# Routing chunks 0 to 5 at the chunk loop's ninth step, with a first tile of expert 0 computed while chunks 6 and 7 are routed

## The reference, cut to what is computed

```python
def moe(x, router_w, router_b, w_gate, w_up, w_down):
    xt = x.reshape(B_ * S_, D_)
    s = jax.nn.sigmoid(xt.astype(jnp.float32) @ router_w.astype(jnp.float32))
    sel = s + router_b.astype(jnp.float32)
    gscore = lax.top_k(sel.reshape(-1, N_GROUPS, EXPERTS_PER_GROUP), 2)[0].sum(-1)
    gidx = jnp.argmax(gscore, axis=-1)
    in_group = (jnp.arange(N_EXPERTS) // EXPERTS_PER_GROUP)[None, :] == gidx[:, None]
    _, eidx = lax.top_k(jnp.where(in_group, sel, -jnp.inf), TOP_K)
    gate = jnp.take_along_axis(s, eidx, axis=1)
    gate = gate / gate.sum(-1, keepdims=True)
    ...
    for e in range(N_EXPERTS):
        hid = jax.nn.silu(xt @ w_gate[e]) * (xt @ w_up[e])
        out = out + combine[:, e:e + 1] * (hid @ w_down[e])
...
x = layer_norm(DEEPNORM_ALPHA * x + y, ln1_w[l], ln1_b[l])   # y: the mixer's output
y = moe(x, router_w, router_b, w_gate[l], w_up[l], w_down[l])
x = layer_norm(DEEPNORM_ALPHA * x + y, ln2_w[l], ln2_b[l])
```

## Time and profile before

| what | value |
| --- | --- |
| median of 3 runs | 950.18 us (949.54 to 957.41) |
| span of the profiled execution | 950.0 us |
| TensorE busy | 925.5 us, 97% of the span |
| VectorE busy | 633.3 us, 67% |
| ScalarE busy | 459.2 us, 48% |
| GpSimd busy | 208.8 us, 22% |
| instructions | 15583 |

### The profile page before, as it was taken

How to read it: one execution, slowest core, us unless ns; L and a number is a source line. 1 busy time by engine, 2 the same in 40 slices (tenths; PEclk the granted TensorE clock), 3 DMA queues, 4 the chain that set the end, 5 groups by cost and what they waited for, 6 DMA issues and landing times.

```text
span 950.0 us, 15583 instructions
## 1 busy us (share of the span) xinstructions
PE 925.5 (97%) x5174; PEld 799.9 (84%) x5174; DVE 633.3 (67%) x965; ACT 459.2 (48%) x631; POOL 208.8 (22%) x229
## 2 busy tenths in 40 slices
PE   8999999999999999999889999999999999999997
PEld 8998887888777788888678898898898898898884
DVE  3433599896328877677874389486689983517487
ACT  4532101010348634532515479476788974536653
POOL 3100000010121000000021543524353642324230
PEclk9999999999999999999999999999999999999997
DMA  8620304111563544445386889879699998838264
GB/s 286 205 96 29 100 33 144 45 45 56 197 216 111 203 157 176 163 156 199 137 308 178 267 285 372 309 252 389 183 372 390 390 390 247 290 67 302 75 223 177
DMA packets 72965, 195.20 MB, mean 205 GB/s; under 512 B 9582, under 2 KB 23488, under 8 KB 72928
## 3 DMA queue, kind: packets, MB, share of 16 engines
q1 hardware_dynamic: 60976, 156.43, 45.0%
q0 software_dynamic: 11808, 38.15, 14.5%
q10 hardware_dynamic: 144, 0.14, 0.1%
HBM read 159.47 MB, written 35.22 MB: 205 GB/s over the span
## 4 chain that ended last, share of the span: by engine, by line
PE 90%; DVE 4%; issue 2%; ACT 2%; DMA 1%; POOL 1%; SPq 0%; POOLq 0%; DVEq 0%; ACTq 0%
PE banks L1294 14%; PE banks L684 14%; PE banks L673 13%; PE banks L699 13%; PE banks L1291 9%; PE banks L1434 9%; PE banks L1358 4%; PE banks L657 2%; PE banks L1466 1%; PE banks L664 1%; PE banks L732 1%; DVE split_weights L1885 1%; PE banks L1412 1%; PE banks L1409 1%; DMA arena<-sum_scratch 1%
## 5 line engine op out<-in xcount | busy, mean ns | idle before, releaser
L766 DVE TENSOR_TENSOR split_weights<-arena,split_weights 128x1024 fp32r<-128x1024 f32 x192 | 223.2, 1219 | 0.0
L762 ACT ACTIVATE split_weights<-arena 128x1024 fp32r<-128x1024 f32 x192 | 190.9, 1056 | 3.8 <-DMA arena<-in_w_down 2.0
L684 PE MATMUL banks<-split_weights,split_rows 128*128 128x256 f32 x1152 | 147.5, 284 | 0.0
L684 PEld LDWEIGHTS banks<-split_weights,split_rows 128*128 128x128 f32 x1152 | 142.7, 191 | 1.9
L1294 PE MATMUL banks<-split_weights 128*128 128x512 f32 (+2 forms) x768 | 136.3, 338 | 1.7 <-DVE split_weights L1742 1.6
L699 PE MATMUL banks<-split_weights,split_hidden 128*128 128x512 f32 x576 | 137.5, 394 | 0.0
L673 PE MATMUL banks<-split_weights,split_rows 128*128 128x512 f32 x576 | 136.2, 393 | 0.7 <-DVE split_rows L949 0.7
L1294 PEld LDWEIGHTS banks<-split_weights 128*128 128x128 f32 x768 | 118.7, 189 | 17.6 <-DVE split_weights L1736 2.1
L673 PEld LDWEIGHTS banks<-split_weights,split_rows 128*128 128x128 f32 x576 | 109.2, 190 | 23.6 <-issue 0.8
L699 PEld LDWEIGHTS banks<-split_weights,split_hidden 128*128 128x128 f32 x576 | 106.5, 188 | 21.6
L587 POOL DMA_INDIRECT sum_scratch<-work,tile_sums x23 | 85.0, 3694 | 110.7 <-ACT work L816 101.8
(11 more groups left out here) (349 smaller groups left out, 1117.0 us busy)
## 6 DMA issues: line engine op xcount, KB each, us to landing
arena<-in_w_gate SPq DMA_DIRECT2D x64, 512.0 KB, 7.2
arena<-in_w_up SPq DMA_DIRECT2D x64, 512.0 KB, 7.1
arena<-in_w_down SPq DMA_DIRECT2D x64, 512.0 KB, 10.0
arena<-in_w_in SPq DMA_DIRECT2D x20, 512.0 KB, 5.3
arena<-in_x SPq DMA_DIRECT2D x16, 512.0 KB, 6.8
arena<-in_w_out SPq DMA_DIRECT2D x8, 512.0 KB, 5.0
x_scratch<-arena SPq DMA_DIRECT2D x8, 512.0 KB, 3.5
sum_scratch<-arena SPq DMA_DIRECT2D x8, 512.0 KB, 4.5
```

The lines of the kernel that those rows point to most:

```text
L684: last = pe.matmul(bank(up_bank[a])[:, 0:DH2], XR[:, hx, k, :], wu[:, hw, k, a * DH2:(a + 1) * DH2], start=(k == 0 and i == 0), stop=(k == ...
L762: act.activation(unit_split(u, 0), unit_slot(u), AF.Copy).then_inc(xw_hi, 1)
L766: dve.tensor_tensor(unit_split(u, 1), unit_slot(u), unit_split(u, 0).bitcast(F32), ALU.subtract).then_inc(xw_lo, 1)
```

## The change

**Ninth step.** ScalarE takes the exponential of the logits of chunks 0 to 5 (AHEAD = T - 2 = 6), and VectorE chooses for these chunks (`choose`, a new function: it finds the two best of four by comparing all pairs, in 25 instructions). TensorE sums the ranks of experts 0 and 1 over these chunks (`first_ranks`) ahead of the router product of chunk 6. VectorE no longer casts `ones`, makes `stri` and subtracts units 2 and 3 in this step: GpSimd does these (its subtraction of units 2 and 3 signals `xw_lo`).

**Tenth step.** VectorE makes the one-hot rows of expert 0's first 128 tokens (`first_one_hots`) ahead of the last residual, and their list `tok1` (`first_indices`) behind it, with TensorE's sum between (`first_tokens`). GpSimd gathers these rows, and subtracts units 4 to 7. ScalarE rounds units 4 and 5 here.

**Behind the loop.** TensorE transposes the gathered rows and multiplies the first tile, outside of the loop over tiles (`first_gate`, `first_up`, `first_hidden`, `first_down`). VectorE splits the rows, then chooses for chunks 6 and 7, and then runs what it ran before behind the choice, with the steps of the first tile set in between (`hidden`, `first_hidden_lo`). TensorE's ranks of all chunks stand between two blocks of the gate product; the sum for expert 0's second tile (`second_tokens`, `tok2`) stands in the up product. GpSimd gathers the second tile when `tok2` is there, and then subtracts units 8 to 11; after these it raises `xw_lo` by 8, gathers the first tile's gates and loads the rows ln2_w and ln2_b. A number `room` is added to the ranks of chunks 6 and 7 where expert 0's first tile isn't full. The one-hot sum stands behind the first tile's down product, and TensorE reads `ntiles` behind it. The loop over tiles begins with tile 1.

The core of the diff (the new functions of TensorE's first tile repeat the products of `body` for tile 0):

```diff
@@ pool_experts
-            pool.wait_ge(x1_out, PRIMED + 32 * T)
+            def first_expert_lo(*units):
+                for u in units:
+                    pool.wait_ge(xw_hi, u + 1)
+                    pool.tensor_tensor(unit_split(u, 1), unit_slot(u), unit_split(u, 0).bitcast(F32), ALU.subtract).then_inc(w_lo, 1)
+            pool.wait_ge(xr_lo, T)
+            pool.tensor_copy(ones_bf, ones[:, :])
+            pool.tensor_tensor(stri, tri[:, :], ident[:, :], ALU.subtract).then_inc(made, 1)
...
+            for i, u in enumerate((2, 3)):
+                pool.wait_ge(xw_hi, i + 1)
+                pool.tensor_tensor(unit_split(u, 1), unit_slot(u), unit_split(u, 0).bitcast(F32), ALU.subtract).then_inc(xw_lo, 1)
+            pool.wait_ge(x1_out, PRIMED + 32 * AHEAD)
             pool.wait_ge(rows_filled, 48)
             pool.wait_ge(first_tok_ready, 1)
+            pool.indirect_dma_start(out=xe, out_offset=None, in_=x1_dram[0:P + AHEAD * P, :],
+                                    in_offset=bass.IndirectOffsetOnAxis(ap=tok1, axis=0)).then_inc(xe_in, 16)
+            pool.tensor_copy(tok_gate, tok1).then_inc(gate_idx_ready, 1)
+            first_expert_lo(4, 5, 6, 7)
+            pool.wait_ge(x1_out, PRIMED + 32 * T)
+            pool.wait_ge(first_tok_ready, 2)
+            pool.wait_ge(xeT_ps, 1)
             pool.indirect_dma_start(out=xe, out_offset=None, in_=x1_dram,
-                                    in_offset=bass.IndirectOffsetOnAxis(ap=tok1, axis=0)).then_inc(xe_in, 16)
-            pool.wait_ge(tok_ready, 1)
-            gather(1)
+                                    in_offset=bass.IndirectOffsetOnAxis(ap=tok2, axis=0)).then_inc(xe_in, 16)
+            pool.sem_inc(idx_ready, 1)
+            first_expert_lo(8, 9, 10, 11)
+            pool.wait_ge(w_lo, PROJECTED + 8)
+            pool.wait_ge(xw_lo, 4)
+            pool.sem_inc(xw_lo, 8)
             pool.wait_ge(gates_out, 16)
...
@@ pe_experts
+            stay_busy(8)
             pe.wait_ge(xe_in, 16)
...
+            stay_busy(10)
+            pe.wait_ge(xw_lo, 4)
+            pe.wait_ge(first_lo, 1)
+            first_gate(range(KC // 2))
+            pe.wait_ge(xe_lo, 1)
+            first_gate(range(KC // 2, KC - 1))
+            ranks()
+            first_gate(range(KC - 1, KC)).then_inc(gate_ps, 1)
+            first_up(0, range(KC // 2))
+            second_tokens()
+            first_up(0, range(KC // 2, KC)).then_inc(up_ps, 1)
+            first_up(1, range(KC // 2))
+            first_hidden(0)
+            first_up(1, range(KC // 2, KC)).then_inc(up_ps, 1)
+            transpose_rows(1)
+            first_hidden(1)
+            first_down(range(FC)).then_inc(y_ps, 1)
             pe.wait_ge(hot_ready, 1)
...
-            pe.wait_ge(xw_lo, 4)
+            pe.wait_ge(ntiles_ready, 1)
+            counts = tile_counts(pe, "pe")
             each_tile(pe, counts, body)
@@ act_experts
+            act.wait_ge(y_ps, 1)
+            act.wait_ge(y_out, ADDED)
+            act.wait_ge(gate_in, 16)
+            act.activation(ys, psum[:, 2:4, :].rearrange("p a n -> p (a n)"), AF.Copy, scale=gate_rows[:, 0:1]).then_inc(y_sb, 1)
@@ VectorE, step of the chunk loop
+                if n == T + 1:
+                    first_one_hots(dve, own)
                 if norms:
                     residual1(ch.plus(-2), 1)
+                    if n == T + 1:
+                        first_indices(dve, own)
...
+                if n == T:
+                    dve.wait_ge(rt_exp, 1)
+                    dve.wait_ge(small_in, 16 * SMALL_LOADS)
+                    choose(dve, own, 0, AHEAD)
                 if projects:
...
-                if n == T:
-                    dve.tensor_copy(ones_bf, ones[:, :])
-                    dve.tensor_tensor(stri, tri[:, :], ident[:, :], ALU.subtract)
-                    for i, u in enumerate((2, 3)):
-                        expert_lo(dve, 0, u, i + 1)
```

289 lines of the change are left out of this document (199 added, 90 removed).

## The result

The changed kernel takes 969.53 us (median of 4 runs, 967.17 to 971.6), the kernel before 953.23 beside it; the ratio is 1.0163 with a 95% interval of 1.0135 to 1.0191. The forecast was 952.0 with a range up to 957. The profiled execution of the changed kernel has a span of 965.8 us, 15.8 more than the 950.0 of before.

A forecast was written before the change was run, and what follows sets the result against it. TensorE, busy 97%, was taken as the bound, so the start S of tile 1's gate product decides: 950.0 + 504.5 - 502.53 = 952.0 us, VectorE and GpSimd taking turns; range 939.5 to 957.

The forecast's parts named there:

- S: Instant at which tile 1's gate product can begin: 502.53 us before, forecast 504.5; the same 23 tiles follow.
- Steps 1 and 2: Choice for six chunks ready at 453.9 us, slowed by GpSimd's units 2 and 3; first tokens tok1 ready at 457.5.
- Step 3: First gather at 459.5 us; unit 4's subtraction delays chunk 7's scaling, which ends at 463.8; unit 5 ends at 465.5.
- Step 4: Chunk 7's transposes and router product take 2.7 us as before, ending at 466.5; first tile's rows split by 470.4.
- Step 5: Choice for two chunks, 3.5 us alone, begins at 470.4 and, slowed by GpSimd's subtractions, is ready at 478.3.
- Step 6: From the second choice to the second tokens 3.5 us: tok2 at 481.9, counts and a tile product done by 484.4.
- Step 7: Second gather 482.8 to 483.9 us, units 8 to 11 until 494.0; VectorE's four small instructions pass one at a time.
- Steps 8 and 9: VectorE's remaining work to the last one-hot at 502.7 us; one-hot sum and counters, 1.74 plus 0.1, give S 504.5.
- The down product: First tile's down product, 5.5 us, waits for the last hidden product until 495.8 and ends at 501.3, just ahead.
- Side by side: Rival, chance 0.25: VectorE and GpSimd don't block each other; S 489.9 or 491.7, 2.6 lost to ln2 load, 940.0 us.
- TensorE stays at 1.2 GHz: Rival, chance 0.12: half clock from waits for ranks and hidden rows until tile 1's first product; 962 us.
- Only one-input instructions are blocked: Rival, chance 0.13: GpSimd's subtractions hold up only VectorE's one-input instructions; S = 494.5, 942 us.

The follow-up runs named there:

- fill: The changed kernel with 12 more TensorE filler products where it waited between 452 and 465 us; ratio to the kernel before 1.0104.
- early: The changed kernel with VectorE's choice for chunks 6 and 7 made ahead of splitting the first tile's rows; ratio to the kernel before 1.0106.
- turns: The changed kernel with GpSimd's units 9 to 11 each waiting until the previous is stored, and unit 6 until 7 is rounded; ratio to before 1.0156.
- fence: The changed kernel with GpSimd copying one column behind the second gather and waiting until it is stored, before unit 8; not timed, profiled span 959.8 us.
- short_all: The changed kernel with each of GpSimd's ten subtractions cut from 1024 to 32 columns; ratio to the kernel before 0.9926.
- gather_last: The changed kernel with GpSimd's second gather moved behind its subtractions of units 8 to 11; not timed, profiled span 974.0 us.
- best3: The changed kernel with units 8 to 11 on VectorE, earlier second choice, 12 fillers, GpSimd's units 2 to 7 later, counters read earlier; ratio to before 0.9976.
- alldve2: The changed kernel with all ten subtractions on VectorE behind what TensorE waits for, earlier second choice, ranks and counters; ratio to the kernel before 0.9940.

## Why the prediction was wrong

**What bounds the kernel: right.** S decided, and the same 23 tiles follow it; the span follows S but for the end and tile 1's clock.

**Steps 1 and 2 (choice, first tokens): right.** Shifted by 0.48 to the clock of the kernel after, the choice was due at 453.4 and came at 453.13, tok1 was due at 457.0 and came at 456.85.

**Step 3 (units 4 and 5, x1): a term too small.** The x1 scaling is two instructions, L2221 x2, and each waited for a subtraction: it ended at 464.88, not 463.3. I had let only the first wait. 1.6 us.

**Step 4 (router, first rows): the largest mistake.** The rows were split at 475.94, due 469.9: 6.0 late. 1.6 are step 3's. Nearly all the rest is TensorE's half clock, which held from 454 to 475: router, fillers and transposes, one behind the other, cost nearly twice what they cost at 2.4 GHz (3.23 against fill's 1.75, 3.60 against 1.96), where the forecast took the price of before, 1.97 for the router. The clock was among the rivals, but only from the ranks on; TensorE's waits begin earlier, at 452. Fill, whose rows were split 4.1 earlier, shows that the clock alone was worth about 4 us.

**Step 5 (second choice): right.** 7.75 us from 475.86 to 483.61, 7.9 forecast, only late by step 4. That it could stand ahead of the rows I did not see; early shows 3.3 to 5.4 us in it.

**Step 6: late by a further us.** tok2 came at 488.17, due 481.4; 0.9 beyond step 5 is the half clock in the up products just ahead.

**Step 7 (turns at units 8 to 11): wrong in kind.** That "each GpSimd subtraction lets one VectorE instruction of that kind through" held for units 2 to 7 and not behind the gather. The end of the last subtraction was due at 493.5 and came at 499.23, 5.7 late: they began at 489.99 instead of 483.4, and took 9.24 together instead of 10.1. What failed is what VectorE had done by then: nothing, so that its last one-hot ended at 512.06, 12.8 us behind the subtractions' end where 8.6 were forecast. One instruction of 9.45 us where four turns had been counted: 4 us, a part of which (in turns and fence all but about 1 us) returns as other waits.

**Steps 8 and 9 (counters, S): too small by 1.7.** The one-hot sum is 0.64 and the stretch of the counters behind it 2.79; I had 1.8 for both.

**The down product** was no bound: it ended at 511.1, ahead of the one-hots. **Tile 1's gate product** was taken at full clock and ran at 1.2 GHz for a part: 1.9.

Together: 5.7 for the end of the subtractions, 4.2 for what was left to do then, 1.7 for the counters, 11.6 in all. S was due at 504.0 on this clock and came 11.5 later.

**The rivals.** *Side by side* had 940.0; short_all, which comes near it, has a span of 942.5 and S at 493.65, with the second gather, 5.18 us, on its chain. The sum without the ports was off by 2.5 us only, but in part by luck: counted from the choice, S came 4.1 us later than its 489.9 (2.4 later than its 491.7), and tile 1's gate product took 8.23 us instead of 5.44; against that, the 2.6 for the ln2 load were not lost, though ScalarE did wait 7.60 us for that load, and the end behind the tiles was 1.3 shorter. The larger part of the mistake lies in the price of the ports and of the clock. *TensorE stays at 1.2 GHz* (962) had the right cause in the wrong place, and I gave it 0.12. *Only one-input instructions are blocked* is refuted, by TENSOR_TENSOR rows of 2.25 and 2.31. The Trainium skill (SBUF — State Buffer, Who interferes with whom) has the loser of the shared ports wait for the winner's whole instruction. The traces agree for units 2 to 7, 1.65 to 2.83 us each; behind a gather the measurement differs, 9.45 us for four instructions, and decides.

## What to carry to other kernels

Work that was moved to GpSimd beside VectorE's small SBUF instructions was paid by VectorE, in full and on the path: ten subtractions, 1.2 us each on VectorE, cost the start of the tiles some 20 us, and taking them back, with the earlier choice, the fillers, the earlier counters and another order, made the same idea 0.6% faster than the kernel before. If GpSimd must work there, let it do so while VectorE waits, reduces or reads PSUM, and not as a row of ready instructions behind a gather; a wait for a semaphore parted them here. And where a step makes TensorE wait, price what it does next at the half clock, above all where it is filler on the path.

## What the runs showed that I had not expected

- Behind an indirect gather, GpSimd's four subtractions that stood ready kept VectorE out for 9.16 to 9.56 us, through all of them, whether the instruction had one input or two, one partition or 128. With a wait for a semaphore behind the gather the same four let one through each, in 1.63 to 2.57 us.
- Some one-input instructions are held as well: TENSOR_SCALAR on 16 and 2 columns took 1.82 and 1.89 us in turns. Others ran on within a subtraction: reductions (0.16 to 0.29 us), reciprocals (0.20, and 0.76 at 445.04 in the kernel after) and instructions on a single column (0.13 and 0.14 in gather_last, 0.21 in best3). So did a product with one operand in PSUM: 0.40.
- The issue of GpSimd's adding scatter takes 1.6 to 2.41 us, or 6.68 to 6.96, in an order that differs between the traces. The last one of the kernel was on the path in alldve2.
